# Order of ScalarE's instructions in the steps of the second attention that turn a dilated tile

## The reference

```python
h = rms_norm(x, norm_mix[l])
proj = h @ w_in[l]
o_a = nsa_mixer(...)             # compressed, selected and window attention, 4 heads
o_b = dilated_mixer(...)         # 3 groups of 2 heads: window w, dilation r
o_c = stick_breaking_mixer(...)  # 6 heads, sigmoid instead of softmax
x = x + cat @ w_out[l]
x = x + square(relu(rms_norm(x, norm_mlp[l]) @ w_up[l])) @ w_down[l]
```

## Time and profile before

| what | value |
|---|---|
| time, median of 3 runs | 1173.74 us (1170.88 to 1173.91) |
| the profiled execution | 1174.21 us, of which the span of its instructions is 1172.4 us |
| PE busy | 1114.2 us, 95% |
| DVE busy | 641.7 us, 55% |
| POOL busy | 529.8 us, 45% |
| ACT busy | 424.9 us, 36% |
| mean granted clock of TensorE | 0.977 |

### The profile page before, as it was taken

One profiled execution on the slowest core, in us unless ns is written; L12 is line 12 of the kernel. 1 busy time (PEld: TensorE's weight loads), 2 busy tenths in 40 slices (PEclk: granted clock), 3 DMA queues, 4 the chain that ended last, 5 costly groups with the idle time before them and its releaser, 6 DMA issues.

```text
span 1172.4 us, 16124 instructions
## 1 busy us (share of the span) xinstructions
PE 1114.2 (95%) x5801; PEld 954.3 (81%) x5801; DVE 641.7 (55%) x1131; ACT 424.9 (36%) x852; POOL 529.8 (45%) x525
## 2 busy tenths in 40 slices
PE   6999999999989999999988987789999999999998
PEld 5788888888779888898888877788878888888887
DVE  6869777677567646485666586735641321321321
ACT  5373668363446532114553565423020110110110
POOL 0000000000443327989454177308976776777772
PEclk9999999999999999999999897699999999999999
DMA  6322322413211002323221000102322223223221
GB/s 249 125 88 90 110 88 93 141 54 126 90 54 37 20 18 73 126 90 127 72 73 55 18 2 18 55 1 91 125 91 97 101 90 108 90 93 104 89 89 54
DMA packets 27280, 97.18 MB, mean 83 GB/s; under 512 B 3024, under 2 KB 3408, under 8 KB 27088
## 3 DMA queue, kind: packets, MB, share of 16 engines
q1 hardware_dynamic: 27216, 96.32, 24.6%
HBM read 94.21 MB, written 2.10 MB: 82 GB/s over the span
## 4 chain that ended last, share of the span: by engine, by line
PE 76%; DVE 12%; ACT 5%; issue 4%; POOL 1%; DMA 1%; SPq 0%; DVEq 0%; POOLq 0%; ACTq 0%
PE bank L1236 21%; PE bank L1238 21%; PE bank L1237 21%; PE bank L788 4%; PE bank L751 3%; PE bank L768 3%; DVE arena L1967 1%; DVE wl L1918 1%; ACT wh L1597 1%; PE bank L810 1%; DVE arena L1021 1%; DMA x<-x_in 1%; POOL wl L1189 0%; DVE arena L2318 0%; DVE arena L939 0%
## 5 line engine op out<-in xcount | busy, mean ns | idle before, releaser
L1185 POOL TENSOR_TENSOR hold<-hold 128x2 f32<-128x2 f32 x117 | 29.3, 251 | 531.2 <-PE bank L1238 531.2
L1236 PE MATMUL bank<-xh,wh 128*128 128x512 f32 x568 | 226.5, 399 | 12.0 <-DVE xl L1887 9.4
L1237 PE MATMUL bank<-xl,wh 128*128 128x512 f32 x568 | 222.0, 391 | 0.0
L1238 PE MATMUL bank<-xh,wl 128*128 128x512 f32 x568 | 221.9, 391 | 0.0
L1236 PE MATMUL bank<-yh,wh 128*128 128x512 f32 x520 | 203.5, 391 | 2.0 <-DVE yl L2323 1.5
L1238 PE MATMUL bank<-yh,wl 128*128 128x512 f32 x520 | 202.6, 390 | 0.0
L1237 PE MATMUL bank<-yl,wh 128*128 128x512 f32 x520 | 202.5, 389 | 0.0
L1189 POOL TENSOR_TENSOR wl<-raw,wh 128x512 fp32r<-128x512 f32 x117 | 175.2, 1498 | 0.0
L1188 POOL TENSOR_TENSOR wl<-raw,wh 128x512 fp32r<-128x512 f32 x117 | 157.1, 1343 | 9.7
L1236 PEld LDWEIGHTS bank<-xh,wh 128*128 128x128 f32 x568 | 107.1, 189 | 35.1 <-issue 11.6
L1186 POOL TENSOR_SCALAR wh<-raw 128x1024 fp32r<-128x1024 f32 x117 | 126.6, 1082 | 0.0
(11 more groups left out here) (260 smaller groups left out, 1856.6 us busy)
## 6 DMA issues: line engine op xcount, KB each, us to landing
raw<-weight_units SPq DMA_DIRECT2D x173, 512.0 KB, 3.4
x<-x_in SPq DMA_DIRECT2D x4, 512.0 KB, 7.6
out_fm<-x SPq DMA_DIRECT2D x8, 256.0 KB, 2.0
arena<-tables SPq DMA_DIRECT2D x1, 1024.0 KB, 10.6
par<-params SPq DMA_DIRECT2D x1, 166.0 KB, 2.4
arena<-swa_table SPq DMA_DIRECT2D x1, 128.0 KB, 11.5
ident<-identity SPq DMA_DIRECT2D x1, 64.0 KB, 8.9
```

Of the source, the lines that this page charges most:

```text
L1185: pool.tensor_tensor(hold[:], hold[:], hold[:], ALU.add).then_inc(held, 1)
L1236: pe.matmul(out, lh, rh, start=start, stop=False)
L1237: pe.matmul(out, lh, rl, start=False, stop=False)
L1238: return pe.matmul(out, ll, rh, start=False, stop=stop)
```

## The change

ACT's copy of the turned dilated tile is put at the head of its step, ahead of `soft1(i + LOOK)`. Nothing else differs: the same instructions with the same operands, waits and signals, and no other engine's program is touched. ACT issues no DMA in these steps.

```diff
                 for i in range(-LOOK, ng + OUT_LAG):
-                    if 0 <= i + LOOK < ng:
-                        soft1(i + LOOK)
-                    if a == 2 and i in TAKEN:
-                        item(TAKEN[i])
-                    if a == 2 and i == F6_HIGH:
-
-                        act.wait_ge(s["scores"], groups[7]["strip0"] + 1)
-                        item(("F", "high"))
-                    if a == 2 and i == SCALES_AT + 1:
-                        item(("scales", 0))
                     if a == 2 and i - 1 in TURNS2:
                         name, m = TURNS2[i - 1]
                         act.wait_ge(*chunk_ready(chunk_of[name, m]))
...
                                        scale=scale).then_inc(chunk_taken(chunk_of[name, m])[0], 1)
+                    if 0 <= i + LOOK < ng:
+                        soft1(i + LOOK)
+                    if a == 2 and i in TAKEN:
+                        item(TAKEN[i])
+                    if a == 2 and i == F6_HIGH:
+
+                        act.wait_ge(s["scores"], groups[7]["strip0"] + 1)
+                        item(("F", "high"))
+                    if a == 2 and i == SCALES_AT + 1:
+                        item(("scales", 0))
                     if 0 <= i + LOOK - 1 < ng:
                         soft2(i + LOOK - 1)
```

More of the change, by code:

```diff
@@ L899, in act_part @@
                 for i in range(-LOOK, ng + OUT_LAG):
+                    if a == 2 and i - 1 in TURNS2:
+                        name, m = TURNS2[i - 1]
+                        act.wait_ge(*chunk_ready(chunk_of[name, m]))
+                        src = B[3 + chunk_of[name, m] % 2][:]
+                        scale = hsc[:, 2:3] if name == "q" else par[:, PC["dil"] + 1:PC["dil"] + 2]
+                        act.activation(doubles[DIL_ORDER.index(TURNS2[i - 1]) % 2].rearrange("p t q -> p (t q)"), src, ACT.Copy,
+                                       scale=scale).then_inc(chunk_taken(chunk_of[name, m])[0], 1)
                     if 0 <= i + LOOK < ng:
@@ L909, in act_part @@
                         item(("scales", 0))
[L910 to L916, removed]
                     if 0 <= i + LOOK - 1 < ng:
```

## The result

The changed kernel takes 1178.49 us, median of 13 runs (1173.29 to 1183.21). The kernel before, run beside it 13 times, takes 1173.57 us. The ratio is 1.0051 [1.0036, 1.0066], which is 6.0 us more (4.2 to 7.7); the two medians lie 4.9 us apart. It is slower, by more than the 3.5 us that the prediction called the limit, and above the range that the prediction gave.

What follows compares the result with a forecast made beforehand. PE was taken to bound the kernel, with 76% of the chain, DVE 12%. Terms 0 + 0 + 0.5 + 0.5 gave +1.0 us on 1173.74, so 1174.7 us, range 1170.8 to 1178.0.

Steps and rivals of the forecast that it cites:

- the 3.5 us that the prediction called the limit: Whole-time difference under 0.3%, or 3.5 us, counted as no change: between 1170.2 and 1177.3 us.
- The waits return nothing: PE's waits for the copy at steps 44 and 50, 1.81 and 2.50 us, pass into PE's next waits; gain 0.
- The first rival: DVE's stream does not hold PE's values(43) and values(49), so all 4.7 us return: 1169.0 us; chance 0.15.
- Group 38: Step 35: soft1(38) starts 0.57 us later, delaying DVE's mask2 and then PE's turn of tile 5; +0.5 us.
- DVE then runs without a stop: From group 38's mask2 to the pair copy ending at 691.38, passing on 0.3 to 0.55 us.
- Group 42: Step 39: the copy waits for PE's turn, mask2(42) moves +1.25 us, 0.75 us are slack; +0.5 us.
- Groups 32 and 48 at nothing: Stick-breaking groups where DVE's mask1, waiting for PE, covers the late soft1; 0, without cover up to 0.57 us each.
- The softmax steps at nothing: A softmax group's soft1 feeds a turn three steps later; several us of slack hide the 0.57 us; cost 0.
- the third rival: POOL's earlier splits meet two-input DVE operations of finish(41) and finish(47): three meetings, 3.8 us, giving 1178.5 us; chance 0.12.
- a change of more than 1 us in DVE's finishes: Sign of a wrong prediction: DVE's finishes more than 1 us longer or shorter in sum.
- The fourth rival: PE's granted clock: one half-speed stretch added or saved, 3.0 us, giving 1177.7 or 1171.7 us; chance 0.16, half each.

Runs made afterwards that it cites:

- The two kernels with steps 43 and 49: Kernel before with the copy first only in steps 43 and 49: POOL at full width 1174.20 us (1.0015), POOL thin 1171.33 us (0.9993).
- POOL thin: POOL's dilated doubling and splits cut to slivers, waits and signals kept; against the full kernel before: old order 1171.76 us (0.9993), changed order 1174.79 us (1.0027).

## Why the prediction was wrong

The order of events came out as forecast. What failed are durations: the sum took DVE's and PE's from the kernel before, and put POOL beside DVE at nothing.

**The waits return nothing: right.** In the changed kernel the two instructions behind the waits take them over:

```profile
711.81 0.41 PE L788 MATMUL bank<-arena 128*128 128x64 f32 x2 [3.25 <-DVE arena L939]
...
727.45 0.66 PE L788 MATMUL bank<-arena 128*128 128x64 f32 x2 [3.55 <-ACT arena L897]
```

They waited 1.18 and 0.28 us before. The forecast increases were 1.8 and 2.4 us; they are 2.07 and 3.27. The two kernels with steps 43 and 49 show it alone. The first rival is out.

**Group 38: the delay right, what it meets wrong.** The step was that `soft1(38)` starts 0.57 us later, which gave +0.5. In the kernel with step 35 alone, whose tile 0 is 1.74 us later than in the kernel before, `mask2` starts 0.57 us later than in the earlier trace rows, as forecast (686.52 less 684.21 less 1.74). Then the scan is 0.88 us longer, and `values(36)` starts 1.45 us later (690.23 less 687.04 less 1.74). PE runs it at the low clock behind the wait (+0.61), the gap to L1080 shrinks by 0.17, and the operation behind that, L1081, takes 1.05 instead of 0.42 us (+0.63). The sum is 0.57 + 0.88 + 0.61 - 0.17 + 0.63 = 2.52, the measured increase at tile 5. In the changed kernel the meetings are others:

```profile
683.61 1.43 DVE L963 TENSOR_SCALAR arena<-arena 128x512 f32<-128x512 f32 x1
...
687.76 0.42 DVE L1020 SCALAR_TENSOR_TENSOR arena<-bank,arena 128x256 f32<-128x256 f32 x1 [0.67 <-ACT arena L861]
688.22 0.87 DVE L1021 TENSOR_TENSOR_SCAN arena<-ones,arena 128x256 f32<-128x256 f32 x1
...
690.76 1.00 PE L788 MATMUL bank<-arena 128*128 128x64 f32 x8
...
692.34 1.08 DVE L1081 TENSOR_TENSOR arena<-arena 128x256 f32<-128x256 f32 x1
```

With 2.26 us for tile 0, `mask2` is 1.29 us later: 0.57 for the swap and 0.7 for L963, held in the step before. The scan adds 0.18, `values(36)` stands at +1.46, L1080 at +1.30, and L1081, held again, adds 0.66: 1.96, against 1.95 measured at tile 5. The step that failed is the sentence "DVE then runs without a stop": its order was kept, and its durations, taken from the kernel before, were not.

**Group 42: the delay right, the sum behind it wrong.** The step was +1.25 for `mask2(42)` less 0.75 of slack. In the kernel with step 39 alone `mask2` is 1.28 us later, the scan 0.86 longer, and the slack is 0.65. PE's turn of group 41 then runs at the low clock, 1.07 us instead of 0.60, and the pair turn comes another 0.48 later. 1.28 + 0.86 - 0.65 + 0.48 = 1.97, as measured. The same for the changed kernel, from these rows, counted from tile 5:

```profile
695.74 1.09 PE L810 MATMUL bank<-ident,arena 128*128 128x128 f32 x4 [1.59 <-DVE yl L1104]
...
696.87 0.69 ACT L905 ACTIVATE arena<-bank,hsc 128x512 f32<-128x512 f32 x1 [1.60 <-PE bank L810]
...
699.15 0.56 DVE L1020 SCALAR_TENSOR_TENSOR arena<-bank,arena 128x384 f32<-128x384 f32 x1 [1.21 <-ACT arena L861]
699.70 1.05 POOL L1144 TENSOR_TENSOR arena<-arena,v 128x512 f32<-128x512 f32 x1
699.74 1.82 DVE L1021 TENSOR_TENSOR_SCAN arena<-ones,arena 128x384 f32<-128x384 f32 x1
...
702.76 0.63 PE L768 MATMUL bank<-ident,arena 128*128 128x128 f32 x4 [1.53 <-DVE arena L939]
```

Here it is PE's turn of tile 5 that runs slowly, 1.09 us against 0.63 (granted clock 0.50 from 695.7 to 697.7 us; before, 0.96 from 691.5 to 692.2), and the copy that ACT now does first has to wait for its end. So `mask2` is 1.28 + 0.46 = 1.74 us later, the scan adds 0.86, the slack takes off 0.65, and 1.95 is left; pair 2 shows 1.97. The terms that were not forecast are the scan beside POOL and 0.5 us of PE at the low clock. The step that failed is the sum behind the delay: it let DVE's scan keep its 0.96 us and PE its speed.

With POOL thin neither is there, and yet 1.49 us are measured. `mask2` is 1.53 us later there (692.61 against 691.99, with tile 0 0.91 us earlier), and no slack takes anything off. What the prediction counted as slack was the gap between DVE's copy and a turn that PE reached late, in a stretch at the low clock. The view by stretches of the kernel before has PE busy all the time from 692 to 695.5 us, at a clock of 0.52:

```profile
692.00:695.50 3.50, 3.50 (x21) 3.50 (x20) 2.53 (x6) 1.88 (x6) 2.21 (x2) 0.52 0.00 0
```

With POOL thin and the old order the same stretch ran at 1.00, and there the turn of group 41 waits for DVE already:

```profile
692.00:695.50 3.50, 3.14 (x25) 2.66 (x24) 2.90 (x7) 1.84 (x7) 1.17 (x3) 1.00 0.00 0
```

```profile
694.77 0.63 PE L768 MATMUL bank<-ident,arena 128*128 128x128 f32 x4 [0.36 <-DVE arena L939]
```

**Groups 32 and 48 at nothing.** They were not run apart. In the changed kernel no turn up to tile 4 shows more than 0.16 us, and from tile 7 to tile 9, which holds group 48's step, it is 0.08 us. The scan of `mask2(48)` was held even so, 0.90 instead of 0.42 us, and this met a stretch in which PE was busy throughout at a clock of 0.50. This agrees with nothing for both.

**The softmax steps at nothing: this failed.** The prediction's reason, "slack of several us", holds for `soft1` itself, as the kernel with POOL thin shows. But the earlier copy also releases POOL earlier, and that was only looked at for one operation of DVE. All DVE instructions between 667 and 725 us that have two SBUF inputs, and L963 and L1069, by shape. First the kernel before (instructions, busy us, mean ns, idle us before them):

```profile
L1081 DVE TENSOR_TENSOR arena<-arena 128x256 f32<-128x256 f32 x4 | 2.9, 715 | 0.1
L1073 DVE TENSOR_TENSOR den<-den,gates 128x4 f32<-128x4 f32 x4 | 2.6, 659 | 0.1
L1021 DVE TENSOR_TENSOR_SCAN arena<-ones,arena 128x512 f32<-128x512 f32 x2 | 2.4, 1224 | 0.1
L1069 DVE TENSOR_SCALAR den<-rsum 128x4 f32<-128x4 f32 x4 | 2.3, 570 | 0.0
L1021 DVE TENSOR_TENSOR_SCAN arena<-ones,arena 128x256 f32<-128x256 f32 x2 | 1.4, 691 | 0.1
L963 DVE TENSOR_SCALAR arena<-arena 128x512 f32<-128x512 f32 x2 | 1.1, 533 | 0.0
L1021 DVE TENSOR_TENSOR_SCAN arena<-ones,arena 128x384 f32<-128x384 f32 x1 | 1.0, 957 | 0.0
L1021 DVE TENSOR_TENSOR_SCAN arena<-ones,arena 128x128 f32<-128x128 f32 x2 | 0.8, 425 | 0.1
```

Then the changed kernel:

```profile
L1081 DVE TENSOR_TENSOR arena<-arena 128x256 f32<-128x256 f32 x4 | 3.1, 763 | 0.1
L1021 DVE TENSOR_TENSOR_SCAN arena<-ones,arena 128x512 f32<-128x512 f32 x2 | 2.8, 1385 | 0.1
L1021 DVE TENSOR_TENSOR_SCAN arena<-ones,arena 128x256 f32<-128x256 f32 x2 | 2.2, 1078 | 0.1
L1069 DVE TENSOR_SCALAR den<-rsum 128x4 f32<-128x4 f32 x4 | 1.9, 475 | 0.0
L963 DVE TENSOR_SCALAR arena<-arena 128x512 f32<-128x512 f32 x2 | 1.9, 930 | 0.0
L1021 DVE TENSOR_TENSOR_SCAN arena<-ones,arena 128x384 f32<-128x384 f32 x1 | 1.8, 1820 | 0.0
L1073 DVE TENSOR_TENSOR den<-den,gates 128x4 f32<-128x4 f32 x4 | 1.5, 383 | 0.1
L1021 DVE TENSOR_TENSOR_SCAN arena<-ones,arena 128x128 f32<-128x128 f32 x2 | 1.3, 662 | 0.1
```

The same 21 instructions take 14.5 us before and 16.5 us after. The operations of `finish` (L1069, L1073, L1081), the only ones that the third rival considered, became 1.3 us shorter: 7.8 to 6.5. The scans grew by 2.5 us, 5.6 to 8.1, and L963 by 0.8. The prediction had also named a change of more than 1 us in DVE's finishes as a sign that it is wrong, and that sign came, with the finishes shorter. So that rival had the right mechanism and the wrong instructions, and its value of 1178.5 us for the time is close to the measured 1178.49 by a coincidence: three meetings in the finishes, which is how it got there, did not happen.

The Trainium skill, GPSIMD Engine Reference, section "Key points", was named in the prediction: POOL and VectorE contend where VectorE has two SBUF inputs or runs in a 2-port perf mode. The scan has two such inputs, so the trace agrees, and the rule should have been applied to it. L963 has one; whether it ran in such a mode, no run here shows. The Trainium skill, SBUF — State Buffer, section "SBUF: two separate sides", says more: whoever starts first has the shared ports for its whole instruction, and the other is blocked. The rows agree in direction both ways, and nearly in size. POOL's L1144 ran from 699.70 to 700.75, and the scan that started 0.04 us behind it took 0.86 us longer, where 1.01 us of POOL's instruction were left. Where the scan came first and had 0.84 us left, POOL's split took 0.63 us longer (693.91, 1.91 us).

**Between tiles 9 and 11,** where the prediction's sum had nothing, 0.75 us arise. PE runs the scores and the turn behind tile 9 more slowly (granted clock 0.50 from 717.9 to 719.6 us; before, 0.65 from 711.7 to 713.0), so DVE comes to its finish 0.34 us later. In the finish L1069 takes 0.53 us more, L1073 0.23 less and L1081 0.47 less. Then the scan of `mask2(51)` meets the split that the copy of step 49 released:

```profile
724.41 1.26 POOL L1157 TENSOR_TENSOR xl<-arena,xl 128x512 fp32r<-128x512 f32 x1
...
724.95 1.28 DVE L1021 TENSOR_TENSOR_SCAN arena<-ones,arena 128x256 f32<-128x256 f32 x1
```

It took 0.69 us in the kernel before, so 0.59 us come here. Together these are the 0.75 us.

**The granted clock.** The fourth rival, a whole stretch at half speed more or less, is not what decided. 2.26 us of the difference of the two profiles are there at tile 0, before the change acts, and nothing is added behind tile 11. Between them the clock has a part of 0.8 us: 0.46 in the slow turn of tile 5 behind its wait of 1.59 us, and 0.34 behind tile 9. (Where one step alone was moved it was 0.61 in `values(36)` and 0.48 in the turn of group 41.)

**The sum.** From tile 0 to tile 11: forecast 1.0 us, measured 4.74. Without POOL's width 1.84 are left: about 0.75 for group 38 and 1.5 for group 42, with 0.4 to 0.6 given back by tile 11. The other 2.9 us come with POOL at full width. The changed kernel's own rows, added up to pair 2, give the same picture without the thin kernels: 0.57 + 1.28 - 0.65 = 1.2 us from the order, 0.70 + 0.18 + 0.66 + 0.86 = 2.4 from the four held instructions of DVE, 0.46 from PE's clock, and 0.16 less for the gap in front of L1080. That is 3.9 us, against 3.92 measured.

**What stays open.** The profiles give 4.7 us and the runs 6.0, with 4.7 inside the interval of 4.2 to 7.7; no run says if there is more than the traces show. Steps 29 and 45 were not moved alone. Step 39 alone has +2.0 us at pair 2 and a ratio of 1.0001. Its profile gives the time back between tiles 7 and 11, where both the meetings with POOL and PE's low-clock stretches fall otherwise, and I did not separate these two. For steps 43 and 49 at full width, 1.0015 [0.9996, 1.0035] leaves it open whether they cost anything.

## What to carry to other kernels

A wait with a name on it is worth what is left after the next wait on the same engine, so read the row behind it first; here two waits of 4.3 us together were worth nothing. When an instruction moves ahead, list also whom it releases, and lay that engine's new times over every instruction of a third engine that it can block, not over the one where the blocking was noticed first. A gap that is seen while PE runs at half its clock, as here at 0.52, is no slack to count on.

## What the runs showed of the hardware

- DVE's scan is held by POOL. A scan of 128x256 took 0.69 us alone and 1.57 us when it started 0.25 us behind POOL's subtraction; one of 128x384 took 0.96 and 1.82 us.
- So is a DVE `tensor_scalar` of 128x512 in float32 with one SBUF input: 0.42 us with POOL thin, 0.57 us in the kernel before, where it started with 0.29 us of POOL's `tensor_scalar` left, and 1.42 us when it started 0.13 us behind POOL's subtraction.
- What the held instruction of DVE loses is what is left of POOL's, less about 0.14 us, in the six cases that I took: left 1.13, 1.02, 1.01, 0.72, 0.32 and 0.29 us, lost 1.00, 0.88, 0.86, 0.59, 0.18 and 0.15 (in this order: L963 with step 33 alone, the scan of group 38 with step 35 alone, the scans of groups 42, 51 and 38 in the changed kernel, and L963 in the kernel before). This gives the price of a meeting from two starts and a duration.
- The hold goes the other way too. POOL's `tensor_scalar` of the split took 1.00 us instead of 0.62 when it started 0.10 us behind DVE's scan of 128x256, and its subtraction 1.91 instead of 1.28 us when it started 0.12 us behind the scan of 128x384.
- A hold appears as a longer duration of the held instruction, not as a wait: the idle time before the changed kernel's eight groups above is 0.0 or 0.1 us. In the list of waits DVE seems undisturbed, and PE's wait is put down to DVE.
- The kernel before already lost time in this way. L1069, L1073 and L1081 take 7.8 us in the stretch above, and with POOL thin 3.1 us (means of 163, 166 and 441 ns). Of these 4.7 us less on DVE, 2.3 are left in the distance from tile 0 to tile 11 (51.28 us against 53.60). The whole time of the thin kernel is 0.9993 [0.9970, 1.0015] of the full one, which is 3.5 us less to 1.8 us more, so it leaves open whether they reach the end.
